# Where a decoder block's first expert gets its token rows: fetched back from DRAM, or picked out of SBUF by one-hot products

## The reference

```
x = x + mixed @ w_out[l]
x = x + moe(rms_norm(x, norm2_g[l]), router_w[l], router_b[l], ...)

def moe(h, ...):                       # T = 512 tokens, 32 experts, TOP_K = 4
    logits = xt @ router_w + router_b
    top_v, top_i = lax.top_k(logits, TOP_K)
    gate = jax.nn.softmax(top_v, axis=-1)
    ...                                # tokens sorted by expert
    hc = xb @ w1[e] + b1[e]            # (rows, 2048), the "up" products
    glu = gt * sigmoid(1.702 * gt)     # gt, up: clipped halves of hc
    y = ((up + 1.0) * glu) @ w2[e] + b2[e]   # the "down" products
    out[token] += gate * y
```

## Time and profile before

| | |
|---|---|
| median of 3 runs | 1600.53 us (1597.37 to 1604.07) |
| the profiled execution's own time | 1599.6 us |
| its span, first to last instruction | 1597.9 us |
| TensorE busy, share of the span | 1535.2 us, 96% |
| VectorE, ScalarE, GpSimd busy | 510.5, 247.4, 308.3 us |
| mean granted TensorE clock | 0.985 of full |
| moved by DMA | 468.16 MB, 293 GB/s over the span |
| expert weights | 384 issues of 1 MB |

### The profile page before, as it was taken

One profiled execution on the slowest core, in us unless ns is written; L12 is line 12 of the kernel. 1 busy time (PEld: TensorE's weight loads), 2 busy tenths in 40 slices (PEclk: granted clock), 3 DMA queues, 4 the chain that ended last, 5 costly groups with the idle time before them and its releaser, 6 DMA issues.

```text
span 1597.9 us, 31850 instructions
## 1 busy us (share of the span) xinstructions
PE 1535.2 (96%) x12965; PEld 650.9 (41%) x12966; DVE 510.5 (32%) x941; ACT 247.4 (15%) x509; POOL 308.3 (19%) x449
## 2 busy tenths in 40 slices
PE   7999999999999789999999999999999999999993
PEld 4655555665445323333334443443333333333331
DVE  4105555342435442223223322422232223322232
ACT  4213343233312101000000100010001000010001
POOL 2000003351100202121222222121212222121101
PEclk9999999999999799999999999999999999999997
DMA  8121131621261789999999999999999999999996
GB/s 235 27 66 40 39 79 27 183 64 30 75 251 53 275 352 399 396 408 409 405 403 408 410 400 408 408 410 398 410 408 410 402 406 408 410 410 398 410 379 207
DMA packets 136093, 468.16 MB, mean 293 GB/s; under 512 B 32663, under 2 KB 74687, under 8 KB 86866
## 3 DMA queue, kind: packets, MB, share of 16 engines
q1 hardware_dynamic: 122258, 446.57, 70.7%
q0 software_dynamic: 13792, 21.00, 6.0%
HBM read 452.41 MB, written 19.29 MB: 295 GB/s over the span
## 4 chain that ended last, share of the span: by engine, by line
PE 76%; DMA 16%; SPq 4%; DVE 2%; issue 1%; ACT 1%; DVEq 0%; PEld 0%; POOL 0%; ACTq 0%; PEldq 0%; POOLq 0%
PE ps L1618 29%; DMA ring<-in_expert_w 15%; PE ps L1225 12%; PE ps L1636 11%; PE ps L1372 7%; PE ps L1640 5%; PE ps L1561 4%; SPq L631 3%; PE ps L1357 2%; PE ps L1334 2%; PE ps L1344 1%; ACT mixT L1028 1%; PE ps L1513 0%; DMA ring<-x 0%; PE ps L1537 0%
## 5 line engine op out<-in xcount | busy, mean ns | idle before, releaser
L1618 PE MATMUL ps<-ring,oT_fox 128*32 128x512 f32 x6144 | 674.4, 595 | 7.1 <-DMA ring<-in_expert_w 7.0
L1618 PEld LDWEIGHTS ps<-ring,oT_fox 128*32 128x32 f32 x6144 | 208.8, 110 | 451.1 <-issue 387.0
L2175 DVE TENSOR_TENSOR mixT<-ps,mask 128x768 f32<-128x768 f32 x64 | 61.0, 953 | 698.4 <-PE ps L1618 698.4
L1636 PE MATMUL ps<-ring,hT 128*32 128x512 f32 x2048 | 269.1, 593 | 0.9 <-DMA ring<-in_expert_w 0.6
L1640 PE MATMUL ps<-ring,hT 128*32 128x256 f32 x2048 | 159.5, 379 | 0.0
L1372 PE MATMUL ps<-hT,ring 128*128 128x512 f32 x304 | 137.0, 597 | 0.0
L1640 PEld LDWEIGHTS ps<-ring,hT 128*32 128x32 f32 x2048 | 70.7, 110 | 149.0 <-issue 149.0
L1152 ACT ACTIVATE mixT<-mixT 128x768 f32<-128x768 f32 x32 | 27.1, 846 | 622.5 <-DVE mixT L2179 622.5
L848 POOL DMA_INDIRECT oT_nsa<-table,pc x93 | 97.4, 1047 | 47.4 <-POOL pc L843 28.0
L868 POOL COPY pT<-pT 96x32 bf16 (+1 forms) x64 | 14.9, 235 | 397.8 <-ACT hT L1162 388.7
L1225 PE MATMUL ps<-hT,ring 128*128 128x512 f32 x208 | 90.4, 593 | 0.2 <-ACT hT L958 0.2
(11 more groups left out here) (301 smaller groups left out, 1119.7 us busy)
## 6 DMA issues: line engine op xcount, KB each, us to landing
ring<-in_expert_w SPq DMA_DIRECT2D x384, 1024.0 KB, 26.1
ring<-in_w_in SPq DMA_DIRECT2D x28, 512.0 KB, 5.1
ring<-in_w_out SPq DMA_DIRECT2D x8, 512.0 KB, 9.4
ring<-in_w_in SPq DMA_DIRECT2D x1, 2144.0 KB, 12.8
xs<-in_x SPq DMA_DIRECT2D x4, 512.0 KB, 4.7
ring<-in_w_in SPq DMA_DIRECT2D x8, 256.0 KB, 3.6
ring<-in_w_proj_nsa SPq DMA_DIRECT2D x16, 128.0 KB, 2.8
ring<-in_w_proj_fox SPq DMA_DIRECT2D x8, 256.0 KB, 3.1
```

The costliest lines, as they stand in the source:

```text
L1618: ins = pe.matmul(wide(ps[TG * j:TG * j + TG, g, :]), xT[b][:, g, c, :], up_slab(c, j), start=(c == 0), stop=(c == NK - 1), tile_position= ...
L1636: pe.matmul(ps[TG * q:TG * q + TG, 4, :], gT[b][:, q // 2, c, :], ring[:, NK + j, at:at + 512], start=False, stop=(c == NK - 1), tile_posi ...
L2175: return dve.tensor_tensor(to, half, b_up[:, 256 * n:256 * n + 256].unsqueeze(1).broadcast_to([P, NG, 256]), ALU.add)
```

## The change

Expert 0's rows no longer go through DRAM. For each token tile t VectorE writes `first_hot` (128 tokens x 96 slots), which holds the norm's factor `rs2` where the token sits in that slot of expert 0 (`mark_first`). TensorE multiplies the x2 rows in SBUF with it, eight chunks of 128 columns for each of the four tiles, 32 products in all (`pick_first`), and these accumulate in PSUM banks 3 and 4 to what `xT` wants; the x2 chunk is the stationary operand and is read with a stride of eight elements. The products of tiles 0 to 2 stand at places where TensorE is between steps of the last tile's routing. Parts 0, 1 and 2 of the last tile's table are filled after c = 0, 1 and 2 of up(0), spread_slots runs after c = 3, and up(0) writes banks 5 to 7. VectorE's order after `shift` is: take_first_x, marks of parts 1 and 2, take_parts, take_quarters, weigh, count_extra. SyncE issues the four w2 slabs of expert 0 together and no longer waits for the gather. GpSimd gathers for experts 1 and 2 one right after the other.

```
@@ SyncE
             sp.wait_ge(out_full, 2 * NT)
-            load_slab(0, NK)
+            for c in range(NK, 12):
+                load_slab(0, c)
             store_table(NT - 1)
-            sp.wait_ge(xg_loaded[0], 16)
             store_x2(NT - 1)
-            for c in range(NK + 1, 12):
-                load_slab(0, c)
@@ GpSimd
-            pool.wait_ge(idx_ready, 1)
-            pool.wait_ge(table_stored, 16 * (NT + 1))
-
-            pool.indirect_dma_start(out=xg[0][0:CAP, :], out_offset=None, in_=table_d,
-                                    in_offset=bass.IndirectOffsetOnAxis(ap=idx_x[0:CAP, 0:1], axis=0),
-                                    bounds_check=S - 1, oob_is_err=False, engine_sem=gather_sent).then_inc(xg_loaded[0], 16)
...
-            pool.wait_ge(idx_ready, 2)
-            now_gather(1, 1)
-            take(now_ready, 1)
-            gathered(1)
+            pool.wait_ge(idx_ready, 1)
+            pool.wait_ge(table_stored, 16 * (NT + 1))
+            for e in (1, 2):
+                now_gather(e, e % 2)
+                take(now_ready, e)
+                gathered(e % 2)
@@ TensorE
+            def pick_first(t, c, end):
+
+                pe.wait_ge(first_marked, t + 1)
+                every = xs[:, t, :].rearrange("p (m c) -> p c m", c=NK)
+                for k in range(c, end):
+                    ins = pe.matmul(first_x(k, k + 1), every[:, k, :], first_hot[:, t, :], start=(t == 0 and k % 4 == 0),
+                                    stop=(t == NT - 1), skip_group_check=True)
+                    if t == NT - 1 and k % 4 == 3:
+                        ins.then_inc(xT_full, 1)
+
+            pick_first(0, 0, 4)
             turn_x2(2 * NT - 1)
+            pick_first(0, 4, 7)
             route(2 * NT - 1)
+            pick_first(0, 7, NK)
+            pick_first(1, 0, NK)
+            pick_first(2, 0, 2)
             count_earlier(NT - 1)
-            for part in range(len(HOT_PARTS)):
-                fill_table(NT - 1, part)
+            pick_first(2, 2, NK)
+            pick_first(NT - 1, 0, NK)
...
-                    if isinstance(e, int) and e == 0 and c == 0:
+                    if not before and c < len(HOT_PARTS):
+                        fill_table(NT - 1, c)
+                    if not before and c == len(HOT_PARTS):
+                        pe.wait_ge(parts_taken, 1)
                         spread_slots()
...
-                if not before:
-                    pe.wait_ge(parts_taken, 1)
-                up(b, lambda c: pe.wait_ge(slab_loaded[c], 16 * e + 16), used)
+                up(b, lambda c: pe.wait_ge(slab_loaded[c], 16 * e + 16), used, HC if before else HC_FIRST)
...
-            pe.wait_ge(count_taken, 1)
-            turn_first_x()
@@ VectorE
+            def mark_first(t):
+
+                dve.tensor_scalar(first_hot[:, t, :], slot_no, placed_at[:, t, 0:1], rs2[:, t:t + 1], ALU.is_equal, ALU.mult)\
+                   .then_inc(first_marked, 1)
...
                 place(t)
+                if t == NT - 1:
+                    step.link(dve.tensor_copy(count, routed(t, 2)))
+                mark_first(t)
                 if t:
                     dve.wait_ge(table_full, t)
                 mark(t, 0)
...
             shift(NT - 1)
-            take_first()
-            mark(NT - 1, 1)
-            dve.wait_ge(gather_sent, 1)
-            mark(NT - 1, 2)
-            dve.tensor_copy(count, routed(NT - 1, 2)).then_inc(count_taken, 1)
-            take_parts()
...
             take_first_x()
+            for part in range(1, len(HOT_PARTS)):
+                mark(NT - 1, part)
+            take_parts()
+            take_quarters()
             weigh(NT - 1)
-            take_quarters()
             count_extra()
             expert(0, 0, gather)
```

More of the change, by code:

```diff
@@ L396, in hybrid_block @@
         quarter_at = pc_f[:, 104:105]
+        first_hot = rope_cos[:, 0:NT * CAP].rearrange("p (t s) -> p t s", t=NT)
         table_quarter = table_d.rearrange("a (q d) -> (a q) d", q=4)
@@ L401, in hybrid_block @@
         gf_b = xs[:, 0, :]
-        hc_g, hc_u = ps[:, 0:NG, 0:256], ps[:, 0:NG, 256:512]
+        HC, HC_FIRST = 0, BANKS - NG
+        hc_g, hc_u = ([ps[:, at:at + NG, 256 * n:256 * n + 256] for at in (HC, HC_FIRST)] for n in range(2))
         y_ps = ps[:, 4:6, :].rearrange("p a b -> p (a b)")[:, 0:768]
@@ L420, in late_of, with first_x @@
         def late_of(e, end):
-            return ps[0:CAP, 5, 3 * e:3 * end].rearrange("p (e v) -> p e v", v=3)
+            return ps[0:CAP, 4, 384 + 3 * e:384 + 3 * end].rearrange("p (e v) -> p e v", v=3)
+        def first_x(c, end):
+            return ps[:, 3 + c // 4, (c % 4) * CAP:(c % 4 + end - c) * CAP]
         b_up = mask[:, :]
@@ L467, in hybrid_block @@
         xg_taken = sem("xg_taken")
-        count_taken = sem("count_taken")
+        first_marked = sem("first_marked")
         spread_full = sem("spread_full")
@@ L487, in hybrid_block @@
         result = sem("result")
-        gather_sent = sem("gather_sent")
         stored = sem("stored")
@@ L872, in _ @@
                 picked(pick_down, b, b, pick_down_ready)
-            pool.wait_ge(idx_ready, 2)
-            now_gather(1, 1)
-            take(now_ready, 1)
-            gathered(1)
+            pool.wait_ge(idx_ready, 1)
[4 more added lines that the diff above has]
+                gathered(e % 2)
             def block(e, b, more, count):
                 o = 1 - b
-                if isinstance(e, int) and e == 0:
-                    take(xT_full, 2)
-                else:
+                if not (isinstance(e, int) and e == 0):
                     take(xg_taken, e)
@@ L895, in block @@
                     scattered(o, count)
-            block(0, 0, True, 0)
+            block(0, 0, False, 0)
             pool.wait_ge(x2_stored, 16 * (NT + 1))
-            pool.wait_ge(idx_ready, 6)
+            pool.wait_ge(idx_ready, 5)
             with pool.Fori(0, E // 2 - 2) as i:
@@ L1158, in take_y @@
                     act.wait_ge(y_stored[b], 32 * k)
-                act.wait_ge(idx_ready, 6)
+                act.wait_ge(idx_ready, 5)
                 for n, cols in enumerate((slice(0, 512), slice(512, 768))):
@@ L1587, in turned_x @@
                     yield ins
[L1589 to L1593, removed]
             def spread_slots():
@@ L1606, in wide, with up @@
                 return c.rearrange("p (n m) -> p n m", n=2)
-            def up(b, loaded, used):
+            def up(b, loaded, used, hc=HC):
                 for j in range(4):
@@ L1617, in up @@
                         for j in range(4):
-                            ins = pe.matmul(wide(ps[TG * j:TG * j + TG, g, :]), xT[b][:, g, c, :], up_slab(c, j),
+                            ins = pe.matmul(wide(ps[TG * j:TG * j + TG, hc + g, :]), xT[b][:, g, c, :], up_slab(c, j),
                                             start=(c == 0), stop=(c == NK - 1), tile_position=(0, TG * j))
@@ L1674, in second @@
                 else:
-                    pe.wait_ge(idx_ready, 6)
+                    pe.wait_ge(idx_ready, 5)
                 pe.wait_ge(pick_down_ready, e + 1)
@@ L2050, in mark @@
                                   placed_at[:, t, first:end].unsqueeze(2).broadcast_to(wide), ALU.is_equal).then_inc(hot_ready, 1)
-            def take_first():
-                dve.wait_ge(table_full, NT)
-                dve.tensor_scalar(idx_x[0:CAP, 0:1], table_of(0, 1)[:, :, 0], -1.0, float(S), ALU.mult, ALU.add).then_inc(idx_ready, 1)
+            def mark_first(t):
+                dve.tensor_scalar(first_hot[:, t, :], slot_no, placed_at[:, t, 0:1], rs2[:, t:t + 1], ALU.is_equal, ALU.mult)\
+                   .then_inc(first_marked, 1)
             def take_quarters():
@@ L2130, in count_extra @@
             def count_extra():
-                dve.wait_ge(count_taken, 1)
                 step.link(dve.tensor_scalar(many, count, float(CAP), None, ALU.is_gt))
@@ L2147, in count_extra, with scaled @@
                 dve.tensor_copy(extra[:, NX:NX + 1], cum[0:1, E - 1:E]).then_inc(extra_ready, 1)
-            def scaled(b, n, signal):
+            def scaled(b, n, signal, turned):
                 dve.tensor_tensor(xT[b][:, :, 4 * n:4 * n + 4, :].rearrange("p g c m -> p c g m"),
-                                  ps[:, 6 + n, 0:4 * CAP].rearrange("p (c g m) -> p c g m", c=4, g=NG),
+                                  turned.rearrange("p (c g m) -> p c g m", c=4, g=NG),
                                   g2k[:, 4 * n:4 * n + 4].unsqueeze(2).unsqueeze(3).broadcast_to([P, 4, NG, TG]),
@@ L2158, in take_first_x @@
                     dve.wait_ge(xT_full, n + 1)
-                    scaled(0, n, xT_ready)
+                    scaled(0, n, xT_ready, first_x(4 * n, 4 * n + 4))
             def take_x(e, b, landed):
@@ L2187, in expert @@
                 dve.wait_ge(b_up_ready, e + 1)
-                biased(gt_b, hc_g, 0).then_inc(glu_ready, 1)
+                hc = 1 if isinstance(e, int) and e == 0 else 0
```

(9 more changed lines are left out.)

## The result

The changed kernel takes 1604.36 us (median of 17 runs, 1601.71 to 1605.94) against 1599.96 us (17 runs, 1597.02 to 1604.07): ratio 1.0025, 95% interval 1.0017 to 1.0032. It is slower by 4.4 us. The forecast was 1594.0 in a range of 1591 to 1600.5, so both the size and the sign were wrong. By the bound of 0.5% set above it counts as "the same", but with this many runs the loss is clear.

The account below looks back on a forecast made before the run. The weight stream, about 1 us per expert slower than TensorE, was taken to set the end from up(1) on; -6.1 us to up(0), -1.4 inside it and +1.0 for the clock gave -6.5, hence 1594.0 us, range 1591 to 1600.5.

Parts of the forecast that it names:

- The rule that the end moves with up(1): Whole kernel: the end moves by as much as the start of up(1) moves; nothing saved later counts.
- the stride: Picks' weight reads, step of eight: taken as 0.11 us per instruction, bounded by 0.16, which would add 2.5 us.
- signs of being wrong: Picks 0.16 us or more apart; clock 0.50 in 522 to 531; expert 1's transpose awaiting its gather; stream resting after up(1).
- strided weight loads: Rival, chance 0.05: picks' weight loads at 0.32 us, up(1) 8 us later than before, time 1608.8 us.
- The rest of the sum: Path to up(1): -6.1 us to the start of up(0), -1.4 net inside it, +1.0 for the clock.
- Inside up(0): During up(0): 32 table products add 1.4 us, faster first c and bias products save 2.8, net -1.4.
- From the count to up(0): From the count of earlier tokens to up(0): 9.5 us before, 3.8 after, so -5.7 us.
- The covers: Before up(1): VectorE has 1.8 us to spare, expert 1's gather 1.3, so the 5.8 us from up(0) stay.
- The clock: From 521 on: stays up, or falls and costs +1 to +3 us; +1.0 taken as the even chance.

Follow-up runs that it names:

- experiments 6 and 7: Changed kernel plus eight idle VectorE operations ahead of transposing expert 1's rows: 1609.62 us; changed kernel plus six idle products between experts 14 and 15: 1605.38 us.
- experiment 4: Kernel before, gather kept, with up(0) in banks 5 to 7, table parts 1 and 2 filled inside up(0), spread_slots after c = 2: 1602.23 us.

## Why the prediction was wrong, point by point

- **The rule that the end moves with up(1)** held to within 3 us over a move of up(1) by 15 (experiments 6 and 7 and the table).
- **The step that failed is "the stride".** I took 0.11 us for an instruction and bounded it by 0.16; it is 0.238. The bound was read off rows 8 in two wrong moves. The eight transposes there stood 0.16 us apart at the lower level; I let that halve with the clock and double for the second pass of a float32 product. But the strided read does not speed up with TensorE's clock: the pick instructions are 0.238 us apart at 1.00 and 0.240 at 0.50. Unstrided ones do: the router products stand 0.112 apart at 1.00 and 0.213 at 0.50 (start to start in the kernel before; the 0.24 that I took for them has the last one's tail in it). So the stride costs 0.13 us an instruction at the higher level and 0.03 at the lower, and rows 8, taken at the lower level, could hardly show it. Why a transposition took only 0.16 is open. Without the halving the upper bound would have been 0.32, which I reserved for the slow rival. The 64 instructions take 15.2 us instead of 7.0, and on the path to up(0) this is 7.7 us: 531.4 without the stride, 539.1 with it. Two of the prediction's signs of being wrong are there: picks over 0.16 us apart, and the clock at 0.50 before 531.
- **The rival "strided weight loads"** had the mechanism and the sign, at a chance of 0.05. Its price of 8 us of loss assumed 0.32 us; it said that the case decides from about 0.25 us on, and at 0.24 us it lost 4.4 us. The rule of the Trainium skill that I cited beside it spoke against the change, and for a step of eight elements it was right; I gave it no weight in the sum.
- **The rest of the sum** can be checked on the kernel without the stride. Forecast: up(0) near 531, first c in 2.6 us, up(1) near 560, 1594.0. Measured: 531.37, 2.58, 560.70, 1594.73.
- **"Inside up(0)"** was put too low. The 32 table products took 0.27 + 0.63 + 0.81 = 1.71 us instead of 1.40, and each of the three breaks made the next c 2.71 instead of 2.58 us, 0.4 more in all: +2.1 for +1.4.
- **"From the count to up(0)"** counted the gather as 1.47 us and the mark and fill as path. The total of 9.5 us was right, being read end to end, but the split was not (experiment 4).
- **The covers** held. In the kernel without the stride up(1) followed 5.8 us after up(0), with nothing late.
- **The clock** stayed up in that kernel, as the better half of my bound said. In the changed kernel it fell at 529.1, 8 us into strided picks, although TensorE shows as busy without a gap; why it fell is not shown. What the lower level cost there is small up to 538, since the picks take 0.24 us at either level; from up(0) on it costs: its first c took 4.16 us.
- **Left open:** in all four profiles with the changed kernel's code VectorE starts on up(0)'s result 0.7 us after the last product's recorded end, in the other five 0.07 us after. It is not VectorE that is late: SyncE waits for the same signal of TensorE and issues its load at 565.17, with VectorE's start at 565.18, and the chain gives the last four c 11.05 us where the kernel without the stride has 10.36. No run tells why.

## What to carry to other kernels

Before data in SBUF is used as a stationary operand through a strided view, look at the step: here float32 weight loads cost nothing extra at a step of 8 bytes and took twice as long from 16 bytes on. That is so at the higher clock level; a price read at the lower level hides it, so take prices at the level at which the new work will run. Change what the other operand takes instead, here which rows of w1 expert 0's slabs are read from; no cost of it shows in the one kernel that did so. And where a stream of transfers is the slower side of a loop, find the last moment at which it rested: only what moves that moment moves the end.

## What the runs showed of the hardware

- An instruction of a float32 product with a 128-column weight load repeats every 0.112 us at a step of one element, 0.118 at two, 0.234 at four and 0.238 at eight, all at the higher clock level. At the lower one the step of eight takes 0.240 and router products without a stride 0.213.
- A stretch of loads with a step of four or eight did not keep the granted clock at its higher level: it fell 6 to 9 us into them in six of six profiles with such picks, and stayed at 1.00 over 10 us of the unstrided ones in the one profile without.
- The gather of 96 rows of 4 KB took 4.7 us from issue to landing in the kernel before and 4.6 in experiment 4, with the DMA engines otherwise nearly idle.
